# A gated-delta inverse in 32x32 blocks, vector work moved off three waits, and a single-pass sum of squares in retention

## The reference

```
# gated DeltaNet, per chunk: a unit lower triangular system
lower = einsum('bhid,bhjd->bhij', kb, kc) * decay * strict
sol = triangular_solve(eye + lower, rhs, lower=True, unit_diagonal=True)
...
# every head's output: RMSNorm over its 128 columns
y = xf * rsqrt(mean(xf * xf, axis=-1) + NORM_EPS) * gain
```

## Time and profile before

| | us |
|---|---|
| Median of three runs (2894.41 to 2895.54) | 2895.05 |
| The profiled execution | 2895.1 |
| its span, first to last instruction | 2893.2 |
| PE busy | 2853.6 |
| DVE busy | 1636.9 |
| ACT busy | 1051.3 |
| POOL busy | 445.0 |
| PE clock granted, mean share of full speed | 0.997 |

### The profile page before, as it was taken

The page is one execution under the profiler, slowest core; times in us unless marked ns, Lnnn a source line. Parts: engine busy times, 40 slices in busy tenths (PEclk is TensorE's granted clock), DMA queues, the critical chain, the costliest instruction groups (busy, mean ns, idle before and its releaser), DMA issues.

```text
span 2893.2 us, 36752 instructions
## 1 busy us (share of the span) xinstructions
PE 2853.6 (99%) x14096; PEld 2389.2 (83%) x14096; DVE 1636.9 (57%) x1607; ACT 1051.3 (36%) x1139; POOL 445.0 (15%) x453
## 2 busy tenths in 40 slices
PE   8999999999999999999999999999999999999997
PEld 5877888878889988899888888888888888888886
DVE  7434666655454443534434433333333798888888
ACT  5323433432454332423424332232332333333334
POOL 2000222200001122200011223323323200000001
PEclk9999999999999999999999999999999999999999
DMA  5323222232347764423322555555555855555555
GB/s 166 94 80 91 74 62 65 74 80 77 113 127 215 230 213 122 164 87 131 120 98 77 164 175 182 186 176 179 188 177 181 291 218 216 204 217 208 212 208 133
DMA packets 453632, 439.56 MB, mean 152 GB/s; under 512 B 9104, under 2 KB 365488, under 8 KB 453424
## 3 DMA queue, kind: packets, MB, share of 16 engines
q1 hardware_dynamic: 424288, 344.56, 38.9%
q0 software_dynamic: 29264, 93.90, 9.1%
HBM read 360.31 MB, written 75.50 MB: 151 GB/s over the span
## 4 chain that ended last, share of the span: by engine, by line
PE 89%; DVE 3%; issue 2%; DMA 2%; ACT 2%; POOL 2%; SPq 0%; DVEq 0%; POOLq 0%; ACTq 0%
PE slab_ps L844 18%; PE slab_ps L846 18%; PE slab_ps L845 18%; PE down_ps L1401 6%; PE down_ps L1403 6%; PE down_ps L1402 6%; PE down_ps L844 2%; PE mix_ps L845 2%; PE mix_ps L846 2%; PE mix_ps L844 2%; PE down_ps L846 2%; PE down_ps L845 2%; POOL dn_ctt L676 1%; PE mix_ps L893 1%; PE mix_ps L900 1%
## 5 line engine op out<-in xcount | busy, mean ns | idle before, releaser
L844 PE MATMUL slab_ps<-act_hi,w_hi 128*128 128x512 f32 (+2 forms) x2704 | 1023.0, 378 | 14.4 <-DVE act_lo L2072 11.1
L846 PE MATMUL slab_ps<-act_hi,w_lo 128*128 128x512 f32 (+2 forms) x2704 | 1000.3, 370 | 0.0
L845 PE MATMUL slab_ps<-act_lo,w_hi 128*128 128x512 f32 (+2 forms) x2704 | 999.4, 370 | 0.0
L2020 DVE TENSOR_TENSOR w_lo<-w_raw,w_hi 128x2048 fp32r<-128x2048 f32 x200 | 469.5, 2348 | 371.2 <-ACT w_hi L1427 370.7
L844 PEld LDWEIGHTS slab_ps<-act_hi,w_hi 128*128 128x128 f32 (+1 forms) x2704 | 509.8, 189 | 106.9 <-issue 23.1
L846 PEld LDWEIGHTS slab_ps<-act_hi,w_lo 128*128 128x128 f32 (+1 forms) x2704 | 509.1, 188 | 88.0 <-issue 0.6
L845 PEld LDWEIGHTS slab_ps<-act_lo,w_hi 128*128 128x128 f32 (+1 forms) x2704 | 509.8, 189 | 86.5 <-issue 6.3
L1427 ACT ACTIVATE w_hi<-w_raw 128x2048 fp32r<-128x2048 f32 x200 | 382.0, 1910 | 520.7 <-PE slab_ps L846 397.0
L1401 PE MATMUL down_ps<-half_hi,u_slot 128*128 128x512 f32 x896 | 349.5, 390 | 1.2 <-DVE half_lo L2717 1.2
L1403 PE MATMUL down_ps<-half_lo,u_slot 128*128 128x512 f32 x896 | 349.5, 390 | 0.0
L1402 PE MATMUL down_ps<-half_hi,u_slot 128*128 128x512 f32 x896 | 349.4, 390 | 0.0
(11 more groups left out here) (380 smaller groups left out, 3129.2 us busy)
## 6 DMA issues: line engine op xcount, KB each, us to landing
w_raw<-in_w_mlp_up_dram SPq DMA_DIRECT2D x64, 1024.0 KB, 6.7
b<-in_w_mlp_down_dram SPq DMA_DIRECT2D x64, 1024.0 KB, 7.0
w_raw<-in_w_in_dram SPq DMA_DIRECT2D x56, 1024.0 KB, 5.6
u_slot<-u_park SPq DMA_DIRECT2D x112, 512.0 KB, 8.1
w_raw<-in_w_cross_kv_dram SPq DMA_DIRECT2D x32, 1024.0 KB, 6.4
u_park<-u_hi POOLq DMA_DIRECT2D x32, 896.0 KB, 9.3
u_park<-u_lo POOLq DMA_DIRECT2D x32, 896.0 KB, 9.0
w_raw<-in_w_mix_out_dram SPq DMA_DIRECT2D x16, 1024.0 KB, 6.0
```

Source lines behind the costliest of these rows:

```text
L844: mm(ps, wh, xh, start=first, stop=False)
L845: mm(ps, wh, xl, start=False, stop=False)
L846: return mm(ps, wl, xh, start=False, stop=last)
L2020: tt(w_lo[:, slot], w_raw[:, slot], f32(w_hi[:, slot]), ALU.subtract).then_inc(on["slab_lo"], 1)
```

## The change

Three parts.

1. **Delta's levels 1 to 4 in compact blocks.** The four diagonal 32x32 blocks of each of the four tiles are kept as [128, 4, 32]: block g lies on partitions 32g to 32g+31. DVE forms `blk_l` straight from PSUM by four small operations, then level 0, the masked couplings `blk_c` of all four levels (no longer POOL) and a transpose. PE does each of the eight steps as 16 matmuls of a 32x32 stationary block by 16 moving columns, into PSUM at the same 32 partitions; the waits for `dn_x` and `dn_uev` stand one HOP ahead of the matmuls that need them. ACT and DVE handle 64 columns in place of 256, the transpose 128 in place of 512. After level 4 DVE spreads the blocks into `dn_xx` and `dn_xt` (three transposes, four copies), which POOL has zeroed. Levels 5 and 6 stay as they were, one HOP later, with their masks made by DVE; DVE also masks `dn_at` (POOL before).
2. **DVE work moved.** In `delta_first` the clearing and the rows come after the convolutions and silu. In `gla_logits` the second pair's prefix sums go behind the first head's output. In gla's third level PE passes two more HOPs (7 in place of 5).
3. **Retention's sum of squares.** ACT copies the square into a rounded part, DVE makes the rest, PE sums both by two fp32r matmuls in place of one f32 matmul, two HOPs later.

At the start POOL makes small masks (24 copies and a clearing). The diff, cut (`...` marks what is left out):

```diff
...
+    BK, NB = 32, P // 32
...
+            for g in range(NB):
+                r = block_rows(g)
+                for n in range(5):
+                    chain.put(nc.gpsimd.tensor_copy(blk_mask[r, n], lvl_mask[r, 6 - n, r]))
+                chain.put(nc.gpsimd.tensor_copy(blk_ident[r], ident[r, r]))
+            chain.sync()
+            nc.gpsimd.memset(blk_u[:], 0.0).then_inc(on["consts"], 1)
...
@@ -662,21 +686,8 @@
                 for par in range(2):
                     hd = i * 2 + par
-                    pool.wait_ge(on["dn_pair"], hd + 1)
-                    for n in range(7):
-                        if n == 2:
-
-                            pool.wait_ge(on["dn_at"], hd + 1)
-                            nc.gpsimd.tensor_tensor(flat3(dn_at[:]), flat3(dn_at[:]), every_tile(tri_incl[:]),
-                                                    ALU.mult).then_inc(on["dn_masked"], 1)
-                            pool.wait_ge(on["dn_x"], hd * 7 + 1)
-                        if n >= 3:
-                            pool.wait_ge(on["dn_v"], hd * 6 + (n - 2))
-                        lvl = lvl_mask[:, 6 - n]
-                        nc.gpsimd.tensor_tensor(flat3(dn_ctt[:, n % 2]), flat3(dn_lt[:]), every_tile(lvl),
-                                                ALU.mult).then_inc(on["dn_ct"], 1)
-                        if n == 0 or n >= 3:
-                            nc.gpsimd.memset(dn_uu[:], 0.0).then_inc(on["dn_zero"], 1)
+                    for t in (dn_xt, dn_xx, dn_uu):
+                        nc.gpsimd.memset(t[:], 0.0).then_inc(on["dn_zero"], 1)
...
+            def norm_sum(parts=None):
                 pe.wait_ge(on["sq_ready"], heads.at(1))
-                mm(M[1][:], ones[:], sq[:], start=True, stop=True).then_inc(on["norm_sum"], 1)
+                if parts is None:
+                    last = mm(M[1][:], ones[:], sq[:], start=True, stop=True)
+                else:
+                    mm(M[1][:], ones_round[:], parts[:, 0], start=True, stop=False)
+                    last = mm(M[1][:], ones_round[:], parts[:, 1], start=False, stop=True)
+                last.then_inc(on["norm_sum"], 1)
...
                 attend(ret_wt)
-                yield HOP
-                yield HOP
-                yield HOP
-                norm_sum()
+                for _ in range(5):
+                    yield HOP
+                norm_sum(ret_sq)
...
                 turn(M[5], lambda t: tile(k, t), "dn_tok")
-                for _ in range(7):
+                for _ in range(6):
                     yield HOP
-                for n in range(1, 7):
-                    pe.wait_ge(on["dn_ct"], hd * 7 + (n + 1))
+                for n in range(1, 5):
+                    pe.wait_ge(on["dn_x"], hd * 7 + n)
+                    yield HOP
+                    for c in range(NT):
+                        for g in range(NB):
+                            r = block_rows(g)
+                            last = mm(halves_of(M[1][r, c * BK:(c + 1) * BK], n, 0), blk_c[r, n - 1, c],
+                                      halves_of(blk_x[r, c], n, 0), start=True, stop=True)
+                    last.then_inc(on["dn_u"], 1)
+                    yield HOP
+                    pe.wait_ge(on["dn_uev"], hd * 6 + n)
+                    yield HOP
+                    for c in range(NT):
+                        for g in range(NB):
+                            r = block_rows(g)
+                            last = mm(halves_of(M[4][r, c * BK:(c + 1) * BK], n, 1), blk_u[r, n - 1, c],
+                                      halves_of(blk_xt[r, c], n, 1), start=True, stop=True)
+                    last.then_inc(on["dn_v"], 1)
+                    if n in (1, 4):
+                        yield SEG
+                    else:
+                        for _ in range(4 - n):
+                            yield HOP
+
+                yield HOP
+                for n in range(5, 7):
+                    pe.wait_ge(on["dn_ct"], hd * 2 + (n - 4))
                     pe.wait_ge(on["dn_x"], hd * 7 + n)
                     for c in range(NT):
                         last = mm(halves_of(tile(M[2], c), n, 0), tile(dn_ctt[:, n % 2], c),
@@ -1000,9 +1040,7 @@
                         last = mm(halves_of(tile(M[4], c), n, 1)[rows], tile(dn_uu, c)[:, rows],
                                   halves_of(tile(dn_xt, c), n, 1), start=True, stop=True)
                     last.then_inc(on["dn_v"], 1)
-                    if n in (1, 4):
-                        yield SEG
-                    elif n == 5:
+                    if n == 5:
                         yield HOP
                         delta_norms(hd + 1)
                         yield HOP
@@ -1073,7 +1111,7 @@
                 for n in range(9):
-                    for _ in range((7 - 3 * par, 2)[n] if n < 2 else 3 if n % 2 else 5):
+                    for _ in range((7 - 3 * par, 2)[n] if n < 2 else 3 if n % 2 else 7 if n == 2 else 5):
...
+            def norm(parts=None):
                 act.wait_ge(on["o_ready"], heads.at(1))
-                fn(sq[:], M[0][:], ACT.Square).then_inc(on["sq_ready"], 1)
+                square = fn(sq[:], M[0][:], ACT.Square)
+                if parts is None:
+                    square.then_inc(on["sq_ready"], 1)
+                else:
+                    chain.link(square)
+                    fn(parts[:, 0], sq[:], ACT.Copy).then_inc(on["sq_hi"], 1)
...
                 def take_u(n):
                     act.wait_ge(on["dn_u"], hd * 6 + n)
-                    if n < 6:
-                        act.wait_ge(on["dn_zero"], hd * 5 + n)
-                    fn(halves_of(dn_uu[:], n, 0), halves_of(M[2][:], n, 0), ACT.Copy).then_inc(on["dn_uev"], 1)
+                    if n == 5:
+                        act.wait_ge(on["dn_zero"], hd * 3 + 3)
+                    u = blk_u[:, n - 1].rearrange("p c s -> p (c s)") if n < 5 else dn_uu[:]
+                    ps = M[1][:, 0:NT * BK] if n < 5 else M[2][:]
+                    fn(halves_of(u, n, 0), halves_of(ps, n, 0), ACT.Copy).then_inc(on["dn_uev"], 1)
...
+                dve.wait_ge(on["sq_hi"], hd + 1)
+                tt(ret_sq[:, 1], sq[:], f32(ret_sq[:, 0]), ALU.subtract).then_inc(on["sq_ready"], 1)
                 y_out(hd + Y_RET, par, hd + H_RET)
...
                 yield HOP
-                chain.link(v.memset(dn_rows[:].bitcast(F32), 0.0))
-                delta_rows(0)
+                dve.wait_ge(on["consts"], 3)
                 for t in range(2):
                     delta_conv(0, 0, t)
                 delta_silu(0, (0, 1))
+                chain.link(v.memset(dn_rows[:].bitcast(F32), 0.0))
+                delta_rows(0)
                 yield SEG
                 yield HOP
                 delta_conv(0, 0, 2)
@@ -2224,20 +2272,49 @@
                 dve.wait_ge(on["dn_dt"], hd + 1)
                 chain.link(tt(dn_bs[:], dn_bs[:], dn_dt[:], ALU.mult))
                 dve.wait_ge(on["dn_gram"], hd + 1)
-                tt(dn_lt[:], M[2][:], dn_bs[:], ALU.mult).then_inc(on["dn_pair"], 1)
-                tt(dn_at[:], M[3][:], dn_dt[:], ALU.mult).then_inc(on["dn_at"], 1)
+                for g in range(NB):
+                    chain.put(tt(blk_l[block_rows(g)], diagonal(M[2], g), diagonal(dn_bs, g), ALU.mult))
+                chain.sync()
+                over = lambda m: m.unsqueeze(1).broadcast_to([P, NT, BK])
+                couple = lambda n: tt(blk_c[:, n - 1], blk_l[:], over(blk_mask[:, n]), ALU.mult)
+                chain.link(tt(blk_x[:], blk_l[:], over(blk_mask[:, 0]), ALU.mult))
+                chain.link(tt(blk_xt[:], over(blk_ident[:]), blk_x[:], ALU.subtract))
+                couple(1)
+                v.transpose(flat(blk_x), flat(blk_xt)).then_inc(on["dn_x"], 1)
+                for n in range(2, 5):
+                    couple(n)
+                chain.put(tt(dn_lt[:], M[2][:], dn_bs[:], ALU.mult))
+                chain.put(tt(dn_at[:], M[3][:], dn_dt[:], ALU.mult))
...
-
-                dve.wait_ge(on["dn_ct"], hd * 7 + 1)
-                chain.link(tt(flat3(dn_xt[:]), every_tile(ident[:]), flat3(dn_ctt[:, 0]), ALU.subtract))
-                v.transpose(dn_xx[:], dn_xt[:]).then_inc(on["dn_x"], 1)
                 dve.wait_ge(on["dn_eg"], hd + 1)
                 tt(dn_qg, dn_c[:, 0], dn_gb[:], ALU.mult).then_inc(on["dn_qg"], 1)
+
+                def coupling(n):
+                    tt(flat3(dn_ctt[:, n % 2]), flat3(dn_lt[:]), every_tile(lvl_mask[:, 6 - n]), ALU.mult).then_inc(
+                        on["dn_ct"], 1)
+
+                def take_block_v(n):
+                    dve.wait_ge(on["dn_x"], hd * 7 + n)
+                    dve.wait_ge(on["dn_v"], hd * 6 + n)
+                    xt = halves_of(flat(blk_xt), n, 1)
+                    chain.link(tt(xt, xt, halves_of(M[4][:, 0:NT * BK], n, 1), ALU.subtract))
+                    if n < 4:
+                        v.transpose(flat(blk_x), flat(blk_xt)).then_inc(on["dn_x"], 1)
+                        return
```

(58 more changed lines are left out.)

9 lines of the change are left out of this document (4 added, 5 removed).

## The result

| | before | after |
|---|---|---|
| median, us | 2894.98 (2894.41 to 2895.54, 4 runs) | 2878.47 (2877.87 to 2880.95, 4 runs) |
| the profiled execution: time / span | 2895.1 / 2893.2 | 2880.95 / 2879.4 |
| block step (PE piece + slab excess) | 0.89 | 0.57 |

The ratio is 0.9943, interval 0.9932 to 0.9955: 16.5 us less, where 17.0 was forecast. The forecast time is within 0.4 us of the median, but the blocks gave 4 us more than their term, and losses that the prediction didn't name or priced too low took about as much.

A forecast was written before the change was run, and what follows sets the result against it. PE, busy 2853.6 us of the span, was taken as the bound. Terms 4.1 + 2.6 + 1.6 + 2.0 + 6.7 = 17.0 off 2895.1 gave 2878.1 us; range 2871.3 to 2893, leaving out two rivals (0.19).

The forecast's parts named there:

- three waits: Single PE waits that stand out, each for a vector operation or what hangs on one: 2.3, 1.7 and 0.9 us.
- A: delta_first: clearing and rows moved behind the convolutions remove PE's wait at the sums of squares and its slow stretch, -4.1 us.
- E: Delta's 32 block steps on PE: each 0.68 us instead of 0.89, -6.7 us in all (ends -11.5 and +41).
- B: gla: two scans leave the chain ahead of the first `gla_qk`, so its two waits go, -2.6 us.
- who is late next: After delta_first's wait goes, PE's next wait, on `dn_qk`, is just met; 0.2 us given back (bounds 0 and 2).
- C: Retention's sum of squares: two single-pass matmuls at 0.46 us replace an f32 sum at 0.86, four heads, -1.6 us.
- D: Delta's eleven small waits for POOL's mask go, 3.5 us, less 1.5 charged for new waits: -2.0 us.
- Rival 3: Delta levels 4 and 5: DVE's chain binds, each head waits 1.2 us more, total 2883; chance 0.17.
- rival 1: Block steps: 32 records go one at a time, 1.30 us a step, +13.1 us, total 2897.9; chance 0.13.

The follow-up runs named there:

- double: Changed kernel with each of the 32 block steps issued twice over, into the same places: 2886.32 us, +7.9 on the changed kernel.
- order_g: Changed kernel with the two loops of each block step exchanged (block row outside, tile inside): 2889.94 us, +11.5 on the changed kernel.
- unroll: Changed kernel with the delta stage's loop written out on PE's queue alone, no jump back between second and third head: 2877.89 us.
- moves_alone: Kernel before with only the vector work moved in delta_first and gla, including gla's two more HOPs: 2893.31 us, ratio 0.9993.
- ret_alone: Kernel before with only retention's sum of squares as two single-pass matmuls, two HOPs later: 2894.07 us, ratio 0.9998.
- whole_again: The changed kernel run once more, nothing altered: 2877.64 us, ratio 0.9941 against the kernel before.
- order_back: Changed kernel with delta_first's order as before (clearing and rows first, then convolutions): 2882.00 us, +3.5 on the changed kernel.
- blocks_alone: Changed kernel with the moved DVE work and retention's new sum undone, keeping the 32x32 blocks and DVE's masks: 2884.23 us, ratio 0.9963.
- coupling_pool: Changed kernel with the masks of delta's levels 5 and 6 made by POOL again instead of DVE: 2875.86 us, -2.6 on the changed kernel.

## Why the prediction was right, point by point

- **Bound.** PE's queue was the bound and stayed it. The change was found as PE groups and PE waits, to within 0.4 us. The prediction's three waits are those that the change can reach; PE's list of before has others as long, the largest of them at the kernel's start, and this one stayed (10.9 us for `act_lo` after):

```profile
PE slab_ps L844 <- DVE act_lo L2072: 11.1, 1, 11.1
PE slab_ps L844 <- DVE w_lo L2020: 1.4, 1, 1.4
PE down_ps L1401 <- DVE half_lo L2717: 1.2, 1, 1.2
```

- **A, -4.1:** the trace gave 4.3, undoing it 3.5. Its parts were read as one: 2.5 us is the wait, the other 1.7 a slow clock that two of four profiles show. That nothing else was late next held only thanks to part E; without the blocks the same edit, with part B's, was worth 1.5, since the wait for `dn_xx` came in its place. The prediction asked who is late next and looked at `dn_qk`, one step short.
- **B, -2.6:** the two waits gave 2.9. The step that failed is "the moved scans follow a head's output and are next read by the second pair, a slab later: nothing". Their own reader was in no hurry, but on DVE's queue the eviction, the clamp and, through ACT, the next square stand behind them: 1.7 us. Net -1.2.
- **C, -1.6:** measured 1.6 by its pieces; alone it gave 0.7, which the noise doesn't tell from 0 or from 1.6. Its trace has 1.1 us of the same wait for `dn_xx`.
- **D, -2.0:** 3.9 removed (3.5 taken) and 2.2 new (1.5 taken): net -1.7. The place was named rightly, level 5 waiting for DVE; PE loses 0.5 to 0.6 us there in each head, where the sum had it 0.3 us ahead.
- **E, -6.7:** measured -10.5; the term was mis-sized. Four row groups do go side by side. By double's split the records cost 0.29, which is what the prediction had for them with its 0.06 for imperfect overlap, and the switch cost 0.28, not the 0.40 of the groups in the earlier trace rows: the fixed term was the one mis-sized. It depends on the order of the loops: with the four row groups not next to each other the step cost 1.01 and the whole 2889.9. The prediction priced the form and said nothing of the order.
- **Not foreseen:** the loop's length on PE's queue (1.1 to 1.6 us), and the slow stretch at 557 us in some executions (1.6).
- The forecast met the median because E's 3.8 too little stood against 1.7 at gla, 1.1 to 1.6 at the jump and 0.3 in D. That these cancel is luck; the mechanisms of all five parts were found, but a forecast within 0.4 us isn't their merit. Rival 3's mechanism (new waits at level 5) took place at 2.2 us; rival 1, no overlap, is what order_g makes of this kernel: 2889.9 measured, where the rival had 2897.9.

## What to carry to other kernels

Small blocks on the diagonal pay on TensorE if consecutive matmuls go to different 32-row groups: put the row group in the innermost loop, and price a step as turns of four (0.035 us here, for 16 or 32 columns) plus about 0.3 for going in and out. When a step is moved off the critical path, list what stands behind it on its own queue, not only who reads it; and when a wait is removed, look whether a second wait stands within its shadow, for then the edit is worth little alone. Count the instructions of a loop's body before multiplying them.

## What the runs showed of the hardware that was not expected

- A matmul of a 32x32 block costs its row group the same for 16 and for 32 columns (0.57 and 0.58 us a step), and four row groups run at once, but only if they are next to each other on the queue (0.57 against 1.01).
- The clock can fall with no idle time ahead: at 557 us of the kernel after PE was busy through two groups on 16 and 64 rows, and the stretch has a clock of 0.58. It was at that place, behind the same two groups (at 573 us where the kernel is later), in 4 of 14 profiles (after, unroll, moves_alone, ret_alone), and not in whole_again, the same kernel as after, where the stretch from 556 to 560 us has a clock of 1.00. What decides it stays open.
- The same 2.3 us of idle time was followed by the 1.2 GHz level in two profiles (before, order_back) and by the full clock in two (blocks_alone, ret_alone). In moves_alone 1.8 us of it was followed by the 1.2 GHz level.
- A jump back in PE's queue cost nothing with 1483 records in the loop, 1.1 to 1.6 us with 2251 (whole_again, after).
- A vector operation of 4 elements took 0.88 us beside POOL's mask, and 0.15 without it (coupling_pool, after).
